# Block 2, MLA and sparse attention: values of two heads in turn, and ScalarE's order around the next head's exponentials

## The chip, the cores and the metric

The kernel runs on one NeuronCore of a Trainium2 chip. Its engines are TensorE (PE, matmuls; its weight loads stand apart as PEld), VectorE (DVE), ScalarE (ACT), GpSimd (POOL) and SyncE (SP), which issues DMAs. The engines run their own queues in order and wait for one another by semaphores. The metric is the time of one execution on the device in microseconds (us). Three runs of the kernel before took 2497.37, 2497.81 and 2498.92, median 2497.81.

## What is computed

Two transformer-like blocks of two layers each on 256 tokens of width 1024, all in fp32. Block 2 is the one that the change touches. In each of its layers four branches (MLA, a short convolution, sparse attention or DSA, gated linear attention or GLA) read the normed input; their outputs are merged with gates:

```python
merged = gates[:, :, 0, :] * (branches[0] @ w_branch[l, 0])
for n in range(1, N_BRANCH_2):
    merged = merged + gates[:, :, n, :] * (branches[n] @ w_branch[l, n])
```

MLA and DSA are attentions of four heads with values of width 64. For each head:

```python
s = jnp.einsum('bqhd,bkhd->bhqk', qb, k).astype(jnp.float32) * scale
s = jnp.where(key_pos[None, :] <= qpos[:, None], s, NEG)
p = jax.nn.softmax(s, axis=-1).astype(v.dtype)
return jnp.einsum('bhqk,bkhd->bqhd', p, v)
```

DSA does the same over 64 keys chosen by an index score, here as a mask over all keys; its values are shared by the heads.

## The kernel before

**Weights.** All weight matrices come through a ring of six slabs of eight 128x128 blocks. SyncE loads a slab when TensorE has released the one six places before; ScalarE copies it rounded to fp32r (`feed_slab`, line 879: "hi"), VectorE subtracts to get the rest ("lo", `low_slab`, line 1318; called lowering below), and TensorE multiplies hi by hi, hi by lo and lo by hi (line 456). ScalarE's `feed` stands behind an evacuation and copies up to four slabs ahead of it; VectorE's `low(..., 2)` goes two slabs ahead of the product it is about to read.

**Gate and branch products.** A merge step `merge2(n, j)` is a gate product "mA" (8 blocks, 24 matmuls of 256 columns) and a branch product "mB" (2 blocks, 6 matmuls). ScalarE takes the tanh of mA (`merge_sigmoid2`), then feeds a slab; VectorE multiplies (`merge_two`, lines 1776 and 1779). These products fill TensorE while attention goes through the other engines. In MLA's stage they are those of the convolution branch (n=1), in DSA's those of GLA (n=3), in GLA's those of MLA (n=0). Below, product k stands for the stage's `merge2(n, k)`.

**Attention of a head.** In block 2's MLA stage (and likewise DSA's) four engines share the work of head h:
- TensorE: scores of head h+1 (`attention_scores`), product 2h, transposes of head h's weights (`attention_turn`, waits for VectorE's "w"), product 2h+1, a wait for "tr" (the turned copy), and `values2`: two fp32 matmuls, which the trace shows as four, of 128 input rows and 64 output columns, writing partitions 0-63 (even head) or 64-127 (odd head) of one bank.
- VectorE: `attention_masked(h+1)` (lines 1746 to 1755, or 1750 in DSA), merge 2h, `attention_combined(h+1)` (reciprocal and weights, lines 1761 and 1766; waits for the exponentials and signals "w"), merge 2h+1, and behind an odd head `attention_output` (the split at lines 1304 and 1306). In MLA the GLA decays (lines 1928 to 1939, 1352) stand behind head 0 and their factors (line 1360) behind head 2; no slab is lowered in them.
- ScalarE: `attention_exp(h+1)` (waits for VectorE's "sc"), tanh of product 2h and a feed, `attention_turned(h)` (copy of the transposes to SBUF, whose drain at line 1166 signals "tr"), tanh of product 2h+1 and a feed.

The order is written out by hand in the loops over heads. PSUM has eight banks, and `b2.take` hands them out in turn: a tile gets the bank that was taken eight takes earlier, once its reader has freed it. GLA's values go through `values2` too, one head at a time. SS and SC2 hold two heads, at h % 2.

Of the kernel before, what the change touches and what calls it, by code (L numbers as in the profile page):

```python
# [34 lines left out]
P = 128  # L35
# [6 lines left out]
T2 = SEQ  # L42
# [175 lines left out]
def program(nc, x_meta, w, par1, lb, lam, final1, par2, positions, final2, consts, out, known):  # L218


    with ExitStack() as ctx:
# [139 lines left out]
        VM, a = view(a, 2, MLA_HEADS * 64)  # L361
# [8 lines left out]
        VS, a = view(a, 2, 64)  # L370
# [14 lines left out]
        GV, a = view(a, 2, GLA_HEADS * 64)  # L385
# [64 lines left out]
        def _(pe):  # L450
# [299 lines left out]
                transposes(b2, (kind, "t", h), [(slice(0, P), slice(i * P, (i + 1) * P), w[:, i * P:(i + 1) * P])  # L750
                                                for i in range(3)])

            def values2(kind, h, V):

                key = (kind, "o", h if kind == "g" else h // 2)
                ps = b2.take(pe, key) if h % 2 == 0 or kind == "g" else b2.of(key)
                r = slice(64 * (h % 2), 64 * (h % 2) + 64)
                mm(ps[r, 0:T2], V[:, 0, h * 64:h * 64 + 64] if V is not VS else V[:, 0, :], SS[:, h % 2, 0:T2], True, False)
                mm(ps[r, P:T2], V[:, 1, h * 64:h * 64 + 64] if V is not VS else V[:, 1, :], SS[:, h % 2, T2:3 * P], False, True,
                   b2.filled(key) if h % 2 or kind == "g" else None)  # L760

            def index_scores(i):

# [8 lines left out]
            for layer in range(DEPTH):  # L772
                enter("two", layer)
                products_behind_norm(b2, ("cq0", "cq1", "ckv"), hn2, T2, [s2["hn"].upto(("att", k)) for k in range(KT)],
                                     [s2["hnlo"].upto(("att", k)) for k in range(KT)])
                for key in ("iq0", "iq1", "ik"):
                    product(b2, key, hn2, T2)
                sum_squares(b2, "ss_q", [SQ2[:, i, :] for i in range(2)], T2, [s2["evac"].upto(k) for k in ("cq0", "cq1")])
                sum_squares(b2, "ss_kv", [SQ2[:, 2, :]], T2, [s2["evac"].upto("ckv")])
                for key in ("vsw", "kr"):  # L780
                    product(b2, key, hn2, T2)
                pe.wait_ge(*s2["evac"].upto("vsw"))
                transposes(b2, "vsw_turned", [(slice(0, P), slice(t * P, t * P + 64 + IDX_HEADS), VW[0:64 + IDX_HEADS, t * P:(t + 1) * P])
                                              for t in range(2)])
                index_scores(0)
                for key in ("cb0", "cc0"):
                    product(b2, key, hn2, T2)
                index_scores(1)
                for key in ("cb1", "cc1", "cx0", "cx1", "qs0", "qs1"):
                    product(b2, key, hn2, T2)  # L790
                pe.wait_ge(*s2["cqn"].upto())
                for h in range(MLA_HEADS):
                    product(b2, ("qu", h), [(CQS[0][:, k, :], CQS[1][:, k, :]) for k in range(2)], T2)
                pe.wait_ge(*s2["ckn"].upto())
                for h in range(MLA_HEADS):
                    product(b2, ("ku", h), [CKS], T2)
                token_major([("vu", 0), ("vu", 1)], [CKS])
                product(b2, "ks", hn2, T2)
                pe.wait_ge(*s2["evac"].upto("kr"))
                scores(b2, "kturn", [(slice(0, MLA_QK), slice(0, T2), rotM[0:MLA_QK, 0:MLA_QK], KR[0:MLA_QK, :])])  # L800
                for p in range(2):
                    pe.wait_ge(*s2["evac"].upto(("qu", 2 * p + 1)))
                    scores(b2, ("qturn", p), [(slice(0, MLA_QK), slice(i * T2, (i + 1) * T2), rotM[0:MLA_QK, 0:MLA_QK],
                                               QM[0:MLA_QK, 2 * p + i, :]) for i in range(2)])
                for key in ("glr", "gq", "gk", "gr0"):
                    product(b2, key, hn2, T2)
                pe.wait_ge(*s2["km"].upto())
                attention_scores("m", 0)
                token_major([("gv", 0), ("gv", 1)], hn2)
                pe.wait_ge(*s2["gls"].upto())  # L810
                product(b2, "gl", [GLS], T2)
                product(b2, "gr1", hn2, T2)
                for h in range(MLA_HEADS):
                    if h + 1 < MLA_HEADS:
                        attention_scores("m", h + 1)
                    merge2(1, 2 * h)
                    attention_turn("m", h)
                    merge2(1, 2 * h + 1)
                    pe.wait_ge(*s2["tr"].upto(("m", h)))
                    values2("m", h, VM)  # L820
                pe.wait_ge(*s2["z"].upto())
                for p in range(GLA_HEADS // 2):
                    pair = [(g, slice(32 * g, 32 * g + 32)) for g in (2 * p, 2 * p + 1)]
                    for t in range(2):
                        side_by_side(b2, [(("lv", g, t), level_parts(g, Z2[r, :, :], t, GQ[r, :], GK[r, :])) for g, r in pair])
                        if t == 1:
                            side_by_side(b2, [(("cross", g), [(slice(0, P), slice(0, P), Z2[r, 3, 0:P], Z2[r, 3, P:T2])]) for g, r in pair])
                        merge2(0, 4 * p + t)
                    if p == 1:
                        attention_scores("s", 0)  # L830
                    for g, r in pair:
                        merge2(0, 4 * p + 2 + g % 2)
                        pe.wait_ge(*s2["att"].upto(g))
                        values2("g", g, GV)
                    sum_squares(b2, ("ssg", p), [SQ2[:, p, :]], T2, [s2["sqo"].upto(p)], ones64)
                for h in range(DSA_HEADS):
                    if h + 1 < DSA_HEADS:
                        attention_scores("s", h + 1)
                    merge2(3, 2 * h)
                    attention_turn("s", h)  # L840
                    merge2(3, 2 * h + 1)
                    pe.wait_ge(*s2["tr"].upto(("s", h)))
                    values2("s", h, VS)
                for j in range(KT):
                    merge2(2, j)
                for j in range(KT):
                    product(b2, ("wo", j), [(Y2S[0][:, k, :], Y2S[1][:, k, :]) for k in range(KT)], T2,
                            ready=[s2["yb"].upto(k) for k in range(KT)] if j == 0 else None)
                sum_squares(b2, "ss_ffn", [Q2[:, 0, :], Q2[:, KT - 1, :]], T2,
                            [s2["total"].upto("ffn"), s2["sq"].upto(("ffn", KT - 1))])  # L850
                up = [("ff", j, half) for j in range(FT) for half in range(2)]
                products_behind_norm(b2, up[:3], hn2, T2, [s2["hn"].upto(("ffn", k)) for k in range(KT)],
                                     [s2["hnlo"].upto(("ffn", k)) for k in range(KT)])
                for key in up[3:]:
                    product(b2, key, hn2, T2)
                for j in range(KT):
                    product(b2, ("down", j), [(FF2[0][:, k, :], FF2[1][:, k, :]) for k in range(FT)], T2,
                            ready=[s2["ff"].upto(k) for k in range(FT)] if j == 0 else None)
                sum_squares(b2, "ss_next", [Q2[:, 0, :], Q2[:, KT - 1, :]], T2,
                            [s2["total"].upto("next"), s2["sq"].upto(("next", KT - 1))])  # L860
                stream["n"] += 1

        @block.scalar
        def _(act):
# [321 lines left out]
            for layer in range(DEPTH):  # L1186
# [57 lines left out]
                op(GE[:, :], GE[:, :], ACT.Ln, bias=one)  # L1244
                nc.scalar.drain().then_inc(*s2["gez"].done())
                for h in range(MLA_HEADS):
                    if h + 1 < MLA_HEADS:
                        attention_exp("m", h + 1)
                    merge_sigmoid2(1, 2 * h)
                    attention_turned("m", h)  # L1250
                    merge_sigmoid2(1, 2 * h + 1)
                    if h == 1:
                        act.wait_ge(*s2["zdiff"].upto())
                        op(Z2[:, :, :], Z2[:, :, :], ACT.Exp)
                        nc.scalar.drain().then_inc(*s2["zexp"].done())
# [13 lines left out]
                                     s2["ckn"].upto() if g == 1 else s2["normed"].upto(0))  # L1269
                attention_exp("s", 0)  # L1270
                for h in range(DSA_HEADS):
                    if h + 1 < DSA_HEADS:
                        attention_exp("s", h + 1)
                    merge_sigmoid2(3, 2 * h)
                    attention_turned("s", h)
                    merge_sigmoid2(3, 2 * h + 1)
                for j in range(KT):
                    merge_sigmoid2(2, j)
# [894 lines left out]
```

## Time and profile before

| | us |
|---|---|
| median of three runs | 2497.81 |
| the profiled execution | 2496.82 |
| its span, first to last instruction | 2495.0 |
| TensorE busy (matmuls) | 2354.8 |
| VectorE busy | 1807.5 |
| ScalarE busy | 1308.6 |

The profiled execution's own time is 1.8 above its span. A busy engine is one that executes; waiting instructions aren't busy. TensorE's matmuls overlap one another at their ends, so their busy time isn't a measure of full rate. The granted clock is 1.00 at 2.4 GHz and 0.50 at 1.2 GHz; its mean over the span was 0.982.

### The profile page before, as it was taken

Reading aid. Unit: us, or ns where it says so; the run is one execution under the profiler, and the core shown is the slowest. Engines: PE = TensorE matmul, PEld = TensorE weight load, DVE = VectorE, ACT = ScalarE, POOL = GpSimd, SP = SyncE. Lnnn points to the kernel's source line nnn. Section 1 sums busy time; section 2 is a strip of 40 time slices with the busy share of each in tenths; the row PEclk is TensorE's granted clock in tenths of the full one; section 3 lists DMA queues with packets and bytes.
Section 4 is the critical chain, followed back from the end, with each engine's and each line's share of the span. In section 5 each row is a group of like instructions: output and inputs, shape, how many; then the busy total and the mean of one; then the engine's idle time right before and its main releaser. Section 6 shows DMA issues by size and latency. Waiting matters only on the chain.

```text
span 2495.0 us, 51424 instructions
## 1 busy us (share of the span) xinstructions
PE 2354.8 (94%) x19438; PEld 2260.7 (91%) x19438; DVE 1807.5 (72%) x3521; ACT 1308.6 (52%) x2192; POOL 387.1 (16%) x492
## 2 busy tenths in 40 slices
PE   7999999998999999999998997989999988998998
PEld 6998898898999998899898997978999988888998
DVE  6689857777875689867777875887766558776764
ACT  5655456755544645556755545545443455455443
POOL 0000003626920000002727910000000000000000
PEclk9999999999999999999999998999999999999999
DMA  6433343344554433343344553433545544344553
GB/s 213 161 112 110 111 144 119 119 161 142 173 177 156 166 119 111 105 157 121 118 164 150 181 183 127 148 123 119 169 163 184 186 139 136 124 136 159 179 181 132
DMA packets 100436, 366.67 MB, mean 147 GB/s; under 512 B 11632, under 2 KB 12144, under 8 KB 99824
## 3 DMA queue, kind: packets, MB, share of 16 engines
q1 hardware_dynamic: 100208, 363.53, 43.5%
q8 instruction: 155, 2.54, 0.4%
q14 instruction: 73, 0.60, 0.1%
HBM read 362.44 MB, written 1.05 MB: 146 GB/s over the span
## 4 chain that ended last, share of the span: by engine, by line
PE 61%; DVE 22%; DVEq 5%; ACT 4%; issue 4%; ACTq 1%; DMA 1%; SPq 0%
PE psum L456 61%; DVE ring_lo L1318 5%; ACT arena L866 2%; DVE arena L1360 1%; DVE arena L1352 1%; DVE arena_r L1306 1%; DMA ring<-w 1%; ACT ring_hi L879 1%; DVE arena_r L1304 1%; DVE arena L1540 1%; PE psum L533 1%; DVEq L1804 1%; DVEq L1298 1%; DVE arena L1537 1%; DVE arena L1368 1%
## 5 line engine op out<-in xcount | busy, mean ns | idle before, releaser
L456 PE MATMUL psum<-hn_hi,ring_hi 128*128 128x272 f32 (+2 forms) x3936 | 1161.2, 296 | 47.5 <-ACT hn_hi L866 20.5
L456 PE MATMUL psum<-hn_hi,ring_lo 128*128 128x272 f32 (+2 forms) x3936 | 1132.5, 289 | 0.0
L456 PE MATMUL psum<-hn_lo,ring_hi 128*128 128x272 f32 (+2 forms) x3936 | 1096.2, 286 | 0.0
L1318 DVE TENSOR_TENSOR ring_lo<-ring,ring_hi 128x1024 fp32r<-128x1024 f32 x562 | 688.8, 1234 | 232.9 <-ACT ring_hi L879 191.0
L456 PEld LDWEIGHTS psum<-hn_hi,ring_hi 128*128 128x128 f32 x3936 | 760.1, 193 | 75.1 <-issue 50.3
L879 ACT ACTIVATE ring_hi<-ring 128x1024 fp32r<-128x1024 f32 x684 | 713.7, 1055 | 215.2 <-DMA ring<-w 185.0
L456 PEld LDWEIGHTS psum<-hn_hi,ring_lo 128*128 128x128 f32 x3936 | 760.8, 193 | 0.0
L456 PEld LDWEIGHTS psum<-hn_lo,ring_hi 128*128 128x128 f32 x3936 | 738.7, 191 | 1.6
L866 ACT ACTIVATE arena<-psum 128x272 f32<-128x272 f32 (+8 forms) x736 | 257.3, 367 | 652.0 <-PE psum L456 533.3
L456 PE MATMUL psum<-arena_r,ring_hi 128*128 128x256 f32 (+2 forms) x2996 | 552.6, 285 | 11.3 <-DVE arena L1854 6.4
L2017 POOL TENSOR_TENSOR ring_lo<-ring,ring_hi 128x256 fp32r<-128x256 f32 x488 | 386.9, 829 | 1060.3 <-ACT ring_hi L879 1060.2
L456 PEld LDWEIGHTS psum<-arena_r,ring_hi 128*128 128x128 f32 x2996 | 464.0, 189 | 15.0 <-DVE arena L1854 6.8
L456 PE MATMUL psum<-arena_r,ring_lo 128*128 128x256 f32 (+2 forms) x1498 | 424.1, 283 | 0.0
L456 PEld LDWEIGHTS psum<-arena_r,ring_lo 128*128 128x128 f32 x1498 | 282.6, 189 | 0.0
L456 PE MATMUL psum<-arena 128*64 128x64 f32 (+12 forms) x2464 | 195.3, 265 | 12.8 <-ACTq L1166 11.6
L456 PEld LDWEIGHTS psum<-arena 128*64 128x64 f32 (+6 forms) x2464 | 149.6, 153 | 58.0 <-issue 19.3
L866 ACT ACTIVATE arena<-arena 128x272 f32<-128x272 f32 (+9 forms) x151 | 87.7, 602 | 96.2 <-DVEq L1298 91.3
L1306 DVE TENSOR_TENSOR arena_r<-arena,arena_r 128x256 fp32r<-128x256 f32 (+2 forms) x150 | 81.4, 543 | 12.6 <-issue 1.7
L866 ACT ACTIVATE arena<-arena,small 128x128 f32<-128x128 f32 (+1 forms) x128 | 59.3, 464 | 55.4 <-DVEq L1298 53.2
L866 ACT ACTIVATE arena<-psum,par_sb 128x272 f32<-128x272 f32 (+1 forms) x88 | 49.6, 566 | 55.9 <-PE psum L456 55.7
L533 PE MATMUL psum<-cst,arena 128*128 128x128 f32 (+4 forms) x292 | 50.1, 273 | 27.6 <-ACTq L941 21.0
L456 PE MATMUL psum<-arena,cst 128*128 128x272 f32 (+2 forms) x232 | 71.1, 403 | 4.4 <-ACTq L1266 3.8
(159 smaller groups left out, 1433.0 us busy)
## 6 DMA issues: line engine op xcount, KB each, us to landing
ring<-w SPq DMA_DIRECT2D x684, 512.0 KB, 3.3
cst<-consts SPq DMA_DIRECT2D x1, 1960.0 KB, 14.0
x_sb<-x_meta SPq DMA_DIRECT2D x1, 1088.0 KB, 4.9
out<-x_sb SPq DMA_DIRECT2D x1, 1024.0 KB, 3.9
arena<-lam SPq DMA_DIRECT2D x1, 256.0 KB, 4.2
par_sb<-par SPq DMA_DIRECT2D x1, 193.0 KB, 4.8
pos_sb<-positions SPq DMA_DIRECT2D x1, 128.0 KB, 6.3
cst<-consts SPq DMA_DIRECT2D x1, 65.5 KB, 4.7
```

Of the source, the lines that this page charges most:

```text
L456: i = nc.tensor.matmul(out_, lhsT=lhsT, rhs=rhs, start=first, stop=last)
L533: t = nc.tensor.transpose(ps[rows, cols], src, ident[0:src.shape[0], 0:src.shape[0]])
L866: i = nc.scalar.activation(out_, in_, func, **kw)
L879: nc.scalar.activation(ring_hi[:, slot], ring[:, slot], ACT.Copy).then_inc(slab_hi[k % RING], 1)
L1298: i = V.drain()
L1304: V.tensor_copy(hi, src)
L1306: return V.tensor_tensor(lo, src, hi.bitcast(F32), ALU.subtract)
L1318: V.tensor_tensor(ring_lo[:, slot], ring[:, slot], ring_hi[:, slot].bitcast(F32), ALU.subtract)\
L1352: V.tensor_tensor(zq[:, z, 0:n].rearrange("p (b t s) -> p b t s", t=2, s=s), paired(C, s, n // (2 * s), step + s), paired(C, s, n // (2 * ...
L1360: V.tensor_tensor(d, d, paired(k, s, n // (2 * s), step + s), ALU.mult)
L1368: V.tensor_tensor(Lt[:, :, :], ps[:, 0:7 * HALF].rearrange("p (a b) -> p a b", b=HALF), lvl[:, :, :], ALU.mult)
L2017: i = nc.gpsimd.tensor_tensor(ring_lo[:, part], ring[:, part], ring_hi[:, part].bitcast(F32), ALU.subtract)
```

## The change

`values2` is replaced by two functions. `gla_values(g)` issues for GLA what was issued before. `pair_values(kind, p, V)` takes the bank of a pair and issues the four matmuls of both heads alternately: first half of keys for the even head, for the odd head, second half for the even head, for the odd head; the last one signals. It is called behind every odd head, when the turned copies of both are waited for, and nothing of the values stands behind an even head. On ScalarE the tanh of product 2h with its feed and the turned copy of head h go ahead of the exponentials of head h+1, in MLA and in DSA. VectorE's, GpSimd's and SyncE's orders are the same.

```diff
@@ -750,14 +750,21 @@
                 transposes(b2, (kind, "t", h), [(slice(0, P), slice(i * P, (i + 1) * P), w[:, i * P:(i + 1) * P])
                                                 for i in range(3)])
 
-            def values2(kind, h, V):
-
-                key = (kind, "o", h if kind == "g" else h // 2)
-                ps = b2.take(pe, key) if h % 2 == 0 or kind == "g" else b2.of(key)
-                r = slice(64 * (h % 2), 64 * (h % 2) + 64)
-                mm(ps[r, 0:T2], V[:, 0, h * 64:h * 64 + 64] if V is not VS else V[:, 0, :], SS[:, h % 2, 0:T2], True, False)
-                mm(ps[r, P:T2], V[:, 1, h * 64:h * 64 + 64] if V is not VS else V[:, 1, :], SS[:, h % 2, T2:3 * P], False, True,
-                   b2.filled(key) if h % 2 or kind == "g" else None)
+            def gla_values(g):
+
+                r = slice(64 * (g % 2), 64 * (g % 2) + 64)
+                ps = b2.take(pe, ("g", "o", g))
+                mm(ps[r, 0:T2], GV[:, 0, g * 64:g * 64 + 64], SS[:, g % 2, 0:T2], True, False)
+                mm(ps[r, P:T2], GV[:, 1, g * 64:g * 64 + 64], SS[:, g % 2, T2:3 * P], False, True, b2.filled(("g", "o", g)))
+
+            def pair_values(kind, p, V):
+
+                ps = b2.take(pe, (kind, "o", p))
+                for i, cols, src in ((0, slice(0, T2), slice(0, T2)), (1, slice(P, T2), slice(T2, 3 * P))):
+                    for e in range(2):
+                        h = 2 * p + e
+                        mm(ps[64 * e:64 * e + 64, cols], V[:, i, h * 64:h * 64 + 64] if V is not VS else V[:, i, :], SS[:, e, src],
+                           i == 0, i == 1, b2.filled((kind, "o", p)) if i and e else None)
 
             def index_scores(i):
 
@@ -816,8 +823,10 @@
                     merge2(1, 2 * h)
                     attention_turn("m", h)
                     merge2(1, 2 * h + 1)
-                    pe.wait_ge(*s2["tr"].upto(("m", h)))
-                    values2("m", h, VM)
+                    if h % 2:
+                        for g in (h - 1, h):
+                            pe.wait_ge(*s2["tr"].upto(("m", g)))
+                        pair_values("m", h // 2, VM)
                 pe.wait_ge(*s2["z"].upto())
                 for p in range(GLA_HEADS // 2):
                     pair = [(g, slice(32 * g, 32 * g + 32)) for g in (2 * p, 2 * p + 1)]
@@ -831,7 +840,7 @@
                     for g, r in pair:
                         merge2(0, 4 * p + 2 + g % 2)
                         pe.wait_ge(*s2["att"].upto(g))
-                        values2("g", g, GV)
+                        gla_values(g)
                     sum_squares(b2, ("ssg", p), [SQ2[:, p, :]], T2, [s2["sqo"].upto(p)], ones64)
                 for h in range(DSA_HEADS):
                     if h + 1 < DSA_HEADS:
@@ -839,8 +848,10 @@
                     merge2(3, 2 * h)
                     attention_turn("s", h)
                     merge2(3, 2 * h + 1)
-                    pe.wait_ge(*s2["tr"].upto(("s", h)))
-                    values2("s", h, VS)
+                    if h % 2:
+                        for g in (h - 1, h):
+                            pe.wait_ge(*s2["tr"].upto(("s", g)))
+                        pair_values("s", h // 2, VS)
                 for j in range(KT):
                     merge2(2, j)
                 for j in range(KT):
@@ -1244,10 +1255,10 @@
                 op(GE[:, :], GE[:, :], ACT.Ln, bias=one)
                 nc.scalar.drain().then_inc(*s2["gez"].done())
                 for h in range(MLA_HEADS):
+                    merge_sigmoid2(1, 2 * h)
+                    attention_turned("m", h)
                     if h + 1 < MLA_HEADS:
                         attention_exp("m", h + 1)
-                    merge_sigmoid2(1, 2 * h)
-                    attention_turned("m", h)
                     merge_sigmoid2(1, 2 * h + 1)
                     if h == 1:
                         act.wait_ge(*s2["zdiff"].upto())
@@ -1269,10 +1280,10 @@
                                      s2["ckn"].upto() if g == 1 else s2["normed"].upto(0))
                 attention_exp("s", 0)
                 for h in range(DSA_HEADS):
+                    merge_sigmoid2(3, 2 * h)
+                    attention_turned("s", h)
                     if h + 1 < DSA_HEADS:
                         attention_exp("s", h + 1)
-                    merge_sigmoid2(3, 2 * h)
-                    attention_turned("s", h)
                     merge_sigmoid2(3, 2 * h + 1)
                 for j in range(KT):
                     merge_sigmoid2(2, j)
```

## Rows read from the trace of the kernel before

**Rows 1.** The page: part 1, and the engines in the chain that ended last.
```profile
PE 2354.8 (94%) x19438; PEld 2260.7 (91%) x19438; DVE 1807.5 (72%) x3521; ACT 1308.6 (52%) x2192; POOL 387.1 (16%) x492
...
PE 61%; DVE 22%; DVEq 5%; ACT 4%; issue 4%; ACTq 1%; DMA 1%; SPq 0%
```

**Rows 2.** TensorE's waits: waiter, releaser: us in total, times, longest.
```profile
PE psum L456 <- ACTq L1166: 11.6, 6, 2.4
...
PE psum L456 <- DVE arena_r L1306: 3.6, 4, 1.3
```

**Rows 3.** MLA's stage, layer 0: window, us, busy by engine, clock, DMA.
```profile
1626.80:1669.00 42.20, 34.34 (x251) 31.49 (x251) 32.55 (x72) 21.78 (x38) 0.00 (x0) 0.96 0.34 113
```

**Rows 4.** TensorE's timeline in MLA's stage, layer 0: start, us, instruction [idle before].
```profile
1647.92 1.72 PE L456 MATMUL psum<-arena 128*64 128x256 f32 x8 [2.41 <-ACTq L1166]
...
1650.60 0.58 PE L456 MATMUL psum<-hn_hi,ring_hi 128*128 128x256 f32 x1 [0.96 <-DVE arena_r L1306]
...
1659.71 0.86 PE L456 MATMUL psum<-arena 128*64 128x256 f32 x4
1660.51 0.39 PE L456 MATMUL psum<-hn_hi,ring_hi 128*128 128x256 f32 x1
```

**Rows 5.** ScalarE's timeline, layer 0: MLA's stage, then DSA's.
```profile
1644.76 0.40 ACT L866 ACTIVATE arena<-arena,small 128x128 f32<-128x128 f32 x1 [5.93 <-DVEq L1298]
...
1647.36 0.47 ACT L866 ACTIVATE arena<-psum 128x384 f32<-128x384 f32 x1
...
1719.05 0.40 ACT L866 ACTIVATE arena<-arena,small 128x128 f32<-128x128 f32 x1 [3.36 <-DVEq L1298]
...
1720.18 1.28 ACT L866 ACT_TABLE_LOAD   x1
1721.47 0.38 ACT L866 ACTIVATE arena<-psum 128x256 f32<-128x256 f32 x1
1721.97 1.06 ACT L879 ACTIVATE ring_hi<-ring 128x1024 fp32r<-128x1024 f32 x1
1722.93 0.47 ACT L866 ACTIVATE arena<-psum 128x384 f32<-128x384 f32 x1
```

**Rows 6.** TensorE's timeline, block 1: level products of one tile.
```profile
123.64 1.14 PE L456 MATMUL psum<-arena 128*64 128x64 f32 x30
```

**Rows 7.** TensorE's timeline in DSA's stage: layer 0 twice, layer 1.
```profile
1723.49 1.71 PE L456 MATMUL psum<-arena 128*64 128x256 f32 x8 [1.67 <-ACTq L1166]
...
1736.89 0.39 PE L456 MATMUL psum<-hn_hi,ring_hi 128*128 128x256 f32 x1 [0.85 <-DVE arena_r L1306]
...
2215.04 0.39 PE L456 MATMUL psum<-hn_hi,ring_hi 128*128 128x256 f32 x1 [0.50 <-DVE arena_r L1306]
```

**Rows 8.** VectorE's timeline in MLA's stage: layer 0, the last row layer 1.
```profile
1635.35 0.17 DVE L1761 RECIPROCAL small<-small 128x2 f32<-128x2 f32 x1 [0.20 <-issue]
...
1644.81 1.23 DVE L1318 TENSOR_TENSOR ring_lo<-ring,ring_hi 128x1024 fp32r<-128x1024 f32 x1
...
1646.36 0.42 DVE L1776 SCALAR_TENSOR_TENSOR arena<-arena,psum 128x256 f32<-128x256 f32 x1 [0.32 <-ACTq L1174]
...
1655.97 0.42 DVE L1776 SCALAR_TENSOR_TENSOR arena<-arena,psum 128x256 f32<-128x256 f32 x1 [1.13 <-PE psum L456]
...
1659.89 0.42 DVE L1776 SCALAR_TENSOR_TENSOR arena<-arena,psum 128x256 f32<-128x256 f32 x1 [1.17 <-PE psum L456]
...
1668.38 0.42 DVE L1776 SCALAR_TENSOR_TENSOR arena<-arena,psum 128x256 f32<-128x256 f32 x1 [1.87 <-PE psum L456]
...
2135.97 0.42 DVE L1776 SCALAR_TENSOR_TENSOR arena<-arena,psum 128x256 f32<-128x256 f32 x1 [2.50 <-PE psum L456]
```

**Rows 9.** TensorE's weight loads in GLA's stage, layer 0.
```profile
1684.80 0.19 PEld L456 LDWEIGHTS psum<-hn_hi,ring_hi 128*128 128x128 f32 x1 [0.15 <-DVE ring_lo L1318]
```

**Rows 10.** Behind DSA's first values, layers 0 and 1: columns as rows 3.
```profile
1725.20:1728.60 3.40, 3.40 (x18) 3.40 (x18) 2.98 (x6) 1.86 (x5) 0.00 (x0) 0.54 0.02 5
...
2205.20:2208.20 3.00, 3.00 (x26) 3.00 (x26) 2.58 (x6) 1.67 (x4) 0.00 (x0) 1.00 0.00 0
```

## The prediction

> **What bounds the kernel now.** I read the page first: TensorE (PE) is busy in 94% of the span and most of the chain that ended last is its matmuls [rows 1], so a microsecond is gained only where TensorE stands still or where its own instructions go. The list of waits comes next: TensorE stood 11.6 us, six times, for line 1166, the drain behind ScalarE's copy of turned weights, and 3.6 us, four times, for VectorE's split at line 1306 [rows 2]. I then looked where these fall. All are in the MLA and sparse (DSA) stages of block 2, two layers each, so four stages. In the first, TensorE is busy in 34.34 of 42.20 us [rows 3]: 7.9 us idle. The timeline shows the pattern there: values of a head start after idle 2.41, the product behind them after 0.96 more [rows 4]. In each of the four stages the values of head 0 wait (1.66 to 1.72), and in both MLA stages those of head 1 as well (2.41, 2.42).
>
> ScalarE is why. Its queue has exp(h+1), tanh, a weight slab's copy, then the turned copy. In MLA exp(2) stood 5.93 us for VectorE (masking comes behind its long GLA block), with tanh and turned(1) queued behind it, and turned(1) ran only at 1647.36. In DSA exp(1) came after 3.36 of idling, then table load 1.28, tanh, slab copy, turned(0) at 1722.93 [rows 5].
>
> **The change, part by part.**
>
> *Values.* A head's values now take 0.80 from their first matmul to the next product's first (1659.71 to 1660.51) [rows 4]. Values of heads 0 and 2 leave their place: head 0's takes 0.80 with it (a switch to the score matmuls stays), head 2's 0.80 and the switch in front, 0.09 (start to start 0.21 where products have 0.12). That is 1.69 per stage. Against it a pair is longer than one head. It has 8 passes of 1536 columns. If halves of the array don't overlap: 0.80 is 768 columns plus a switch of 0.17, so 0.82 ns a column, and the pair is 1.26 + 0.17 = 1.43, +0.63. If they do: the level products write partitions 0-63 and 64-127 in turn with all 128 input rows, just as the pair will, and 30 passes of 64 columns took 1.14 with the last one's 0.22 of drain in it [rows 6], 0.031 a pass, 0.48 ns a column, where one behind the other they would be 0.053 and 1.6 in all. So weights of one half load while the other half streams, and the pair is 0.74 + 0.17 = 0.91, +0.11. I take 0.1: same tile shape, same alternation, only wider. Bounds per pair: 0 and +0.63; 8 pairs.
>
> The Trainium skill says otherwise (TensorE: Matmul & The Clock Gate, Part 3, "What overlaps and what doesn't"): weight loads overlap running matmuls only when the row group differs, and the two heads share all rows. By that rule the pair would be the serial one; it is the first rival.
>
> *Waits for turned copies, and the order on ScalarE.* tanh(2h) and turned(h) no longer sit behind exp(h+1). Even heads' waits go with their values. For h=1, tanh(2) can run as its gate product ends, turned(1) behind the transposes: about 1640.4 in layer 0's MLA, and TensorE comes to the pair at 1642.8. No wait; TensorE is first there. The split's waits (0.96, 1.31 [its pattern in layer 0: rows 4], 0.85, 0.50 [rows 7]) were for a PSUM bank: banks go round in eights and gate product 4 got that of pair 0's values. With the pair taken later, product 4 gets the bank of scores 2, freed by masking, and pair 0's bank comes due at product 6's second half. That wait goes as well.
>
> What is late next differs by stage.
>
> *MLA, both layers: VectorE.* It has the long GLA block and no slab is lowered in it; TensorE lives on two slabs of lead. Rolled forward in layer 0, with 2.9 for a gate product (24 matmuls at 0.12), 0.7 for its branch product, 0.25 for transposes, 0.8 for scores with their switch: TensorE leaves product 1 at 1634.5, does scores 2, product 2, turn 1 and product 3 by 1642.8, the pair by 1643.7, scores 3 by 1644.5, and after one block of product 4 stands at the next slab at 1645.0. VectorE lowered that slab from 1644.81 on [rows 8], now 0.6 later (below), so it ends near 1646.6; TensorE waits 1.6 there. From then VectorE is the chain and gains just its old idling: 0.32 + 1.13 + 1.17 + 1.87 [rows 8] + 0.30 at the last split = 4.8. The new order costs it one wait: combined(1) started at 1635.35 [rows 8]; now table load, tanh, slab copy, turned(0) and exp(1) run first (ScalarE is free at 1631.5; 1.28 + 0.4 + 1.1 + 0.5 + 1.1), to 1635.9: 0.6. Net 4.2. In layer 1 the same with 2.50 [rows 8] for 1.13: 5.6. TensorE itself would be 5.7 and 7.3 ahead at the stage's end, but GLA takes this back: in the old trace TensorE already stood 0.15 for a lowering there [rows 9], so that slab has no slack and the gain is VectorE's. The falls of the granted clock in these stages are thereby covered too and I count nothing for them.
>
> *DSA, both layers: TensorE.* Two heads cost it about 9 us, VectorE 7.5 to 8. Rolled forward in layer 0 by the same steps: TensorE leaves product 1 at 1721.7, has scores 2 by 1722.8, product 2 by 1726.5, turn 1 and product 3 by 1730.3. The pair needs turned(1): ScalarE has tanh 2 at 1725.9, a slab copy, and turned(1) by 1727.7, 2.6 early. Turns want w(1) at 1726.5 (VectorE has it at 1723.3) and w(3) at 1743.5 (1739.1). exp(h+1) now starts only after turned(h), 1.5 after the gate product; VectorE is late by more than that with its lowerings, so I find one wait of 0.25 on it, inside TensorE's lead. Layer 0: 1.67 + 0.85 [rows 7] + 1.69 - 0.2 = 4.0, and the clock: after the idling it fell to 1.2 GHz, mean 0.54 for 3.40 us in which 18 matmuls ran, where layer 1 at full clock (2.4 GHz) had 26 in 3.00 [rows 10]; 18 are 2.1, so 1.3 is lost. Without the idling I expect no fall: 5.3. Layer 1, without one: 1.66 + 0.50 + 1.69 - 0.2 = 3.65.
>
> No DMA, slab or table load is added or moved; slab copies stay behind the same tanh, up to a few us earlier, and the slab transfers follow TensorE's releases, earlier by what TensorE gains.
>
> **Sum.** 4.2 + 5.6 + 5.3 + 3.65 = 18.8. Span 2495.0 - 18.8 = 2476.2; the profiled execution took 1.8 more than its span, 2478.0, and the median of the runs shown is 1.0 above that execution: 2479.0.
>
> **Rivals.**
> 1. *The pair doesn't overlap* (it doesn't do what it says). In MLA +0.63 hides behind VectorE; in DSA 4 pairs cost 0.53 more than counted: 2481.1. The level products speak against it, unless long streams behave otherwise.
> The Trainium skill's rule on weight loads, named above, would give that time too.
> 2. *Idle moves and the clock falls elsewhere.* MLA has a new wait of 1.6 beside narrow matmuls, and TensorE meets VectorE anew in GLA. A fall costs 1.3 to 1.5 if nothing covers it. Two to four falls more, with VectorE's later waits not all absorbed (half of MLA's 9.8 lost): 2479 + 4.9 + 4 = 2488. For it: falls already sit behind such idling [rows 10]. Against: total idling shrinks.
> 3. *Slower: VectorE waits at every combined(h+1).* exp(h+1) now ends about 3.2 after the gate product, VectorE's merge at 1.8 if it is prompt; so it waits 1.4, lowers its next slab that much later, and if TensorE has no lead, stands for it. Three heads, four stages: 12 x 1.4 = 16.8 lost, with the gain consumed by the same chain: 2497.8 + 16.8 = 2514.6. It decides where VectorE comes to combined less than 1.4 behind the merge and TensorE's lead is under one slab. Rows 8 show VectorE idling before merges 4, 5 and 7, that is prompt, in the old order; but there its lead was two slabs, and once TensorE stops waiting VectorE isn't prompt.
> 4. *Unseen gain*: neither the 0.6 in MLA nor pair cost, and one clock fall elsewhere goes: 2476.
>
> **How the numbers follow.** Forecast with its neighbours (2475 to 2483): 0.58, within it; rival 1: 0.12; rival 2: 0.15; rival 4 or beyond (down to 2472): 0.08; rival 3 whole or in part: 0.07, of which 0.04 ends slower. About 0.2% (5.0 us) is what a measurement here can tell from no change. Faster than 2492.8 has the forecast, rivals 1, 2 and 4, less a hundredth of rival 2: 0.92; within it 0.04; slower 0.04. The range reaches to rival 2's end and a little under rival 4: 2473 to 2489.
>
> **What would show it.** Line 1166 gone from TensorE's list of waits, or near; values as eight matmuls with their starts in pairs a few ns apart, four times in each layer; line 1306 not releasing product 4; in MLA VectorE with next to no idling between the GLA block and pair 1, and TensorE's idling there named after ring_lo (line 1318); granted clock 1.00 at DSA's start in layer 0. Wrong if the starts of a pair's matmuls are 0.2 apart throughout, if VectorE shows waits for ScalarE line 1159 in all heads, or if TensorE idles as much as before under other names.

## The result, and the profile after

The changed kernel took 2478.64 us (median of four runs, 2478.29 to 2480.0) beside 2498.36 for the kernel before on the same chip: ratio 0.992, 95% interval 0.9903 to 0.9938, 0.8% or 19.7 us faster. The profiled execution's span is 2476.9 against 2495.0. Forecast were 2479.0 and 18.8 us. Lines behind the edit on TensorE's side stand 11 further down (L1166 is now L1177, L1306 is L1317, L1318 is L1329, L1159 is L1170).

The page of the changed kernel, part 1 and the engines of the chain, answers to [rows 1]:

```profile
PE 2345.0 (95%) x19438; PEld 2253.9 (91%) x19438; DVE 1806.4 (73%) x3521; ACT 1306.9 (53%) x2192; POOL 386.6 (16%) x492
...
PE 60%; DVE 23%; DVEq 6%; ACT 4%; issue 4%; DMA 1%; ACTq 1%; SPq 0%
```

In TensorE's list of waits both rows of [rows 2], the turned copy's and the split's, are gone. In their place the waits for a lowered slab have grown (before: 20.1 us, 19 times), and there is a small new one, for the masking:

```profile
PE psum L456 <- DVE ring_lo L1329: 26.9, 25, 3.3
...
PE psum L456 <- DVE arena L1758: 0.4, 2, 0.2
```

TensorE's timeline in MLA's stage, layer 0, answers to [rows 4]. All its idling from the transposes of head 0 to GLA stands in it: a slab (1.58, the same as before the change), the bank of scores 2 (0.21), product 4's second slab (1.43). The windows view behind it has the first pair alone (the ninth matmul of x9 is the end of the product before):

```profile
1634.24 0.39 PE L456 MATMUL psum<-hn_hi,ring_hi 128*128 128x256 f32 x1 [1.58 <-DVE ring_lo L1329]
...
1643.67 1.72 PE L456 MATMUL psum<-arena 128*64 128x256 f32 x12
...
1645.60 0.39 PE L456 MATMUL psum<-hn_hi,ring_hi 128*128 128x256 f32 x1 [0.21 <-DVE arena L1758]
...
1647.65 0.39 PE L456 MATMUL psum<-hn_hi,ring_hi 128*128 128x256 f32 x1 [1.43 <-DVE ring_lo L1329]
```

```profile
1643.66:1644.46 0.80, 0.80 (x9) 0.49 (x8) 0.80 (x4) 0.00 (x0) 0.00 (x0) 1.00 0.57 225
```

VectorE and ScalarE there, for [rows 8] and [rows 5]: one wait for exp(1), 1.27; behind the GLA block VectorE's merges have no idling in front (pair 1's starts at 1665.67), and turned(1) runs at 1640.82, ahead of the 5.02 that exp(2) stands for masking:

```profile
1636.92 0.17 DVE L1772 RECIPROCAL small<-small 128x2 f32<-128x2 f32 x1 [1.27 <-ACTq L1170]
...
1646.37 1.23 DVE L1329 TENSOR_TENSOR ring_lo<-ring,ring_hi 128x1024 fp32r<-128x1024 f32 x1
1647.51 0.41 DVE L1787 SCALAR_TENSOR_TENSOR arena<-arena,psum 128x256 f32<-128x256 f32 x1
...
1655.90 0.41 DVE L1787 SCALAR_TENSOR_TENSOR arena<-arena,psum 128x256 f32<-128x256 f32 x1
...
1663.32 0.41 DVE L1787 SCALAR_TENSOR_TENSOR arena<-arena,psum 128x256 f32<-128x256 f32 x1
```

```profile
1640.82 0.47 ACT L877 ACTIVATE arena<-psum 128x384 f32<-128x384 f32 x1
1646.31 0.40 ACT L877 ACTIVATE arena<-arena,small 128x128 f32<-128x128 f32 x1 [5.02 <-DVEq L1309]
```

GLA's slab, for [rows 9] (TensorE's weight loads; the matmul behind it shows 0.77), and DSA's start in layer 0 at full clock, for [rows 10]:

```profile
1681.38 0.19 PEld L456 LDWEIGHTS psum<-hn_hi,ring_hi 128*128 128x128 f32 x1 [0.97 <-DVE ring_lo L1329]
```

```profile
1718.36:1721.76 3.40, 3.40 (x26) 3.07 (x26) 2.91 (x8) 1.90 (x2) 0.00 (x0) 1.00 0.45 159
```

**By stages.** Both traces hold the same 16,410 product matmuls in the same order, so the start of one in a trace less its start before is how far that kernel is ahead there, and the change of this over a stage is what the stage gained. This is worked out from the starts, for the changed kernel and every experiment (us; negative is faster):

```
                      MLA 0  GLA 0  DSA 0  MLA 1  GLA 1  DSA 1    sum   time  before  ratio (95%)
changed               -5.20  +0.80  -5.91  -6.57  +0.79  -4.07 -20.16 2478.64 2498.36 0.9920 (0.9903-0.9938)
e9_changed_again      -5.21  +0.83  -5.89  -6.90  +1.12  -4.07 -20.12 2479.27 2499.44 0.9924 (0.9910-0.9938)
e1_pairs_only         -1.08  +0.01  -5.59  -3.43  -0.01  -3.75 -13.85 2488.53 2496.09 0.9968 (0.9956-0.9980)
e2_order_only         +0.22  -0.01  -2.77  -0.96  -0.02  -0.94  -4.48 2495.15 2496.09 0.9995 (0.9986-1.0004)
e3_head_by_head       -5.20  +0.77  -5.89  -6.60  +0.78  -4.05 -20.19 2479.18 2496.09 0.9927 (0.9913-0.9940)
e4_exp1_before_feed   -6.59  +1.11  -5.91  -7.98  +1.08  -4.07 -22.36 2482.18 2496.09 0.9940 (0.9925-0.9955)
e10_exp1_again        -6.59  +1.13  -5.91  -7.95  +1.13  -4.08 -22.27 2476.80 2499.44 0.9912 (0.9899-0.9926)
e5_mla_only           -5.20  +0.78  -1.48  -6.91  +1.11  -0.01 -11.71 2488.24 2498.48 0.9962 (0.9946-0.9977)
e6_dsa_only           +0.08  +0.01  -5.88  -0.93   0.00  -4.09 -10.81 2488.17 2498.48 0.9959 (0.9944-0.9974)
e7_even_twice         -5.50  +1.11  -4.51  -6.89  +1.12  -2.67 -17.34 2485.76 2498.48 0.9947 (0.9932-0.9962)
e8_gpsimd_lowers      -6.32  +1.11  -5.89  -7.59  +0.75  -4.07 -22.01 2479.87 2498.48 0.9929 (0.9915-0.9942)
```

Outside these stages the changed kernel's trace lost 1.0 early in block 1, 2.4 between the layers and gained 1.3 behind the last stage, where falls of the granted clock lie in one trace and not in the other: -20.2 + 1.0 + 2.4 - 1.3 = -18.1, the difference of the spans. Where TensorE is the chain and no fall lies in a stage, the stages repeat within 0.04 (DSA layer 1: -4.05 to -4.09 in the seven traces with pairs and order both changed there). MLA alone moves by up to 0.3 between traces of one kernel (layer 1: -6.57 and -6.90), and GLA behind it gives that back (together -5.78 both times). The times, with such falls in them, move by 3, so the experiments are read by stages first. One thing goes into every row of the table: all are compared with the same single trace of before, and falls in that trace count as a gain. Two of them are found below, 1.48 in DSA of layer 0 (e5) and 0.93 in MLA of layer 1 (e6), so of each sum about 2.4 (an estimate from these two entries) isn't shown to be the change's work. Of the 20.2, some 17.8 is left.

### The profile page after: what moved, and what is told of

It reads as the page before. It is cut to its first block, busy times and chain, and to the rows that moved or that the text cites. A ratio compares the mean times of both kernels' runs of the same rounds, so it can differ in the third digit from the quotient of the medians.

```text
span 2476.9 us, 51424 instructions
## 1 busy us (share of the span) xinstructions
PE 2345.0 (95%) x19438; PEld 2253.9 (91%) x19438; DVE 1806.4 (73%) x3521; ACT 1306.9 (53%) x2192; POOL 386.6 (16%) x492
## 4 chain that ended last, share of the span: by engine, by line
PE 60%; DVE 23%; DVEq 6%; ACT 4%; issue 4%; DMA 1%; ACTq 1%; SPq 0%
PE psum L456 59%; DVE ring_lo L1329 5%; ACT arena L877 2%; DVE arena L1371 2%; DVE arena L1363 1%; DMA ring<-w 1%; DVE arena_r L1317 1%; ACT ring_hi L890 1%; DVE arena_r L1315 1%; DVE arena L1551 1%; DVE arena L1379 1%; DVEq L1788 1%; PE psum L533 1%; DVEq L1815 1%; DVEq L1309 1%
## 5 line engine op out<-in xcount | busy, mean ns | idle before, releaser
L1329 DVE TENSOR_TENSOR ring_lo<-ring,ring_hi 128x1024 fp32r<-128x1024 f32 x562 | 688.6, 1233 | 237.7 <-ACT ring_hi L890 196.1
L456 PE MATMUL psum<-arena 128*64 128x64 f32 (+13 forms) x2464 | 188.7, 265 | 1.2 <-ACTq L1053 1.0
L456 PEld LDWEIGHTS psum<-arena 128*64 128x64 f32 (+7 forms) x2464 | 146.4, 154 | 43.1 <-issue 18.6
L1317 DVE TENSOR_TENSOR arena_r<-arena,arena_r 128x256 fp32r<-128x256 f32 (+2 forms) x150 | 81.2, 541 | 12.6 <-issue 1.7
```

The lines of the kernel that those rows point to most:

```text
L456: i = nc.tensor.matmul(out_, lhsT=lhsT, rhs=rhs, start=first, stop=last)
L1317: return V.tensor_tensor(lo, src, hi.bitcast(F32), ALU.subtract)
L1329: V.tensor_tensor(ring_lo[:, slot], ring[:, slot], ring_hi[:, slot].bitcast(F32), ALU.subtract)\
```

## The experiments

Four questions: which half of the change brings what, why a pair costs nothing, which engine sets MLA's end, and whether the clock's fall belonged to the idling.

### e1_pairs_only: TensorE's side alone

```diff
-                    merge_sigmoid2(1, 2 * h)
-                    attention_turned("m", h)
                     if h + 1 < MLA_HEADS:
                         attention_exp("m", h + 1)
+                    merge_sigmoid2(1, 2 * h)
+                    attention_turned("m", h)
```
(against the changed kernel, and the same in DSA)

> TensorE's side of the change alone: values of two heads in one pair behind every odd head, ScalarE's order as before (exponentials of the next head first). Theory (pairs are what helps in DSA, the order what helps in MLA): in DSA the pair needs only turned(1), which ScalarE has some 1.5 us before TensorE gets there even behind exp(2), so no wait for line 1170's copy there and DSA gains as in the whole change, 5.9 in layer 0 and 4.1 in layer 1. In MLA exp(2) stands for the masking behind VectorE's long GLA block with turned(1) behind it, so TensorE waits at pair 0 until about the same moment as before, 5 us or more in one piece; only the wait for the split and the values of head 2 are gained, about 2 per layer. Sum 14, time 2484.5. Rival (ScalarE's order is the main part in all stages): DSA keeps waits for turned copies at the pairs, gains under 2 per stage, time 2491 or more. Rival (the order adds nothing, pairs are all): 2479, as the whole change.

The sum was -13.9, 14 expected; the time was 2488.53, 4.0 above the expected 2484.5. In DSA TensorE waits 0.26 and 0.25 for a turned copy, so the order of ScalarE is worth 0.3 a stage there. In MLA it stands 5.19 in one piece behind product 3, as foreseen. TensorE's timeline of this kernel, layer 0's MLA and DSA:

```profile
1645.60 3.13 PE L456 MATMUL psum<-arena 128*64 128x256 f32 x12 [5.19 <-ACTq L1177]
...
1727.21 1.72 PE L456 MATMUL psum<-arena 128*64 128x256 f32 x12 [0.26 <-ACTq L1177]
```

Per stage I was off in MLA: 1.1 gained in layer 0 where 2 were expected, 3.4 in layer 1. In layer 0 more of the stage ran at 1.2 GHz, mean granted clock 0.87 (0.96 before, [rows 3]); windows view of that stage:

```profile
1624.50:1662.70 38.20, 31.77 (x225) 30.24 (x226) 30.86 (x70) 20.49 (x36) 0.00 (x0) 0.87 0.33 111
```

The time, 7.6 less than before, fell short of the stages' sum: the trace lost 4.7 between the layers, and gained 2.3 ahead of the first MLA stage.

### e2_order_only: ScalarE's side alone

```diff
-                    if h + 1 < MLA_HEADS:
-                        attention_exp("m", h + 1)
                     merge_sigmoid2(1, 2 * h)
                     attention_turned("m", h)
+                    if h + 1 < MLA_HEADS:
+                        attention_exp("m", h + 1)
```
(against the kernel before, and the same in DSA)

> ScalarE's side alone: tanh, feed and turned(h) ahead of exp(h+1), TensorE's values head by head in their old places. Theory: the six waits for turned copies go, but in both layers' MLA product 4 still takes the bank of pair 0's values and waits for VectorE's split, which comes no earlier (VectorE has no idling up to there), so MLA gains nothing or loses 0.5 a layer; DSA layer 0 gains its 1.7 wait and the clock fall behind it, 1.9, DSA layer 1 its 1.7; the 0.9 and 0.5 for the split and all values stay. Sum 4 to 5.3, time 2493 to 2494.5. Rival (the waits for turned copies are the loss, whatever the values do): all 11.6 us of them plus the clock, 2485.

The sum came out as expected, -4.5, but 2.4 of it is the falls in the trace of before that every row shares, which leaves about 2.1. The time says the same: 2495.15 where 2493 to 2494.5 was expected, 0.9 less than before, and the interval of the ratio holds 1. So ScalarE's order alone isn't a gain clear of noise. What holds of the theory is the wait that comes next. The waits for turned copies shrink from 11.6 to 0.6, and the one for the split takes their place, from 3.6 to 13.0. TensorE's list of waits, then its timeline in layer 0's MLA and DSA:

```profile
PE psum L456 <- DVE arena_r L1306: 13.0, 4, 5.4
...
PE psum L456 <- ACTq L1166: 0.6, 2, 0.3
```

```profile
1651.61 0.58 PE L456 MATMUL psum<-hn_hi,ring_hi 128*128 128x256 f32 x1 [5.03 <-DVE arena_r L1306]
...
1735.17 0.39 PE L456 MATMUL psum<-hn_hi,ring_hi 128*128 128x256 f32 x1 [1.28 <-DVE arena_r L1306]
```

So neither half does it alone. The raw sums, 13.9 and 4.5, make 18.3, 1.8 less than the whole, but they hold the 2.4 of before's trace twice. Without it the halves are about 11.4 and 2.1, together 13.5 of 17.8: some 4.2 comes only when both are there. The times on this chip agree in direction (7.6 and 0.9 for the halves, 16.9 for e3, which has both). Taking the pair late is what frees product 4 of the split's bank.

### e3_head_by_head: the order inside a pair

```diff
-                for i, cols, src in (...):
-                    for e in range(2):
-                        h = 2 * p + e
+                for e in range(2):
+                    h = 2 * p + e
+                    for i, cols, src in (...):
```

> The changed kernel, but inside a pair all four passes of the even head come before the four of the odd head. Theory (it is the alternation between partitions 0-63 and 64-127 that makes a pair as short as one head, 0.80): head by head a pair takes about 1.4, +0.6; in MLA that lies inside TensorE's waits for lowered slabs (1.4 behind pair 0, 0.8 in GLA), in DSA it is lost in full, four pairs x 0.6 = 2.4; time 2481. If TensorE were the chain in MLA as well it would be 8 x 0.6 = 4.8: 2483.4. Rival (the order inside a pair doesn't matter, the array takes both halves at once in any order): 0.80 a pair, 2478.6.

My theory fell: all stages are as in the changed kernel. By shapes, the passes that start in the pair's first 0.47 us (1643.63 to 1644.10) and in the rest of it (the line with ring_lo is the end of the product before); columns as in the costliest groups of the page:

```profile
L456 PE MATMUL psum<-arena 128*64 128x256 f32 x4 | 0.7, 405 | 0.0
L456 PE MATMUL psum<-arena_r,ring_lo 128*128 128x256 f32 x1 | 0.3, 279 | 0.0
...
L456 PE MATMUL psum<-arena 128*64 128x128 f32 x4 | 0.4, 273 | 0.0
```

Issued were two passes of 256 columns and two of 128 for the even head, then as many for the odd. Four of 256 start first: the odd head's ran ahead of the even head's 128-wide ones, and its first started 14 ns behind the even head's first. Halves run beside one another whatever the order of issue.

### e7_even_twice: the same half twice

```diff
-                for i, cols, src in (...):
-                    for e in range(2):
+                for e in (0, 0, 1):
+                    for i, cols, src in (...):
```

> The changed kernel, but in every pair the even head's two matmuls are issued twice before the odd head's, the second time over the first. Theory (halves of the array's columns run beside one another in whatever order they are issued, the same half one behind the other): the repeat needs the same half, 768 columns more, so a pair takes 0.80 + 0.6 = 1.4; in MLA the waits for lowered slabs behind the pairs (1.4 and 0.8) hide it, in DSA it is lost: 4 x 0.6 = 2.4, time 2481. Rival (matmuls of 64 output columns overlap whatever half they write): 0.8 a pair, no loss. Rival (TensorE is the chain in MLA as well): 8 x 0.6 = 4.8.

The pair now spans 1.50 (1644.62 to 1646.12), 0.70 more: the same half does queue. Passes that start in the first 0.63 us, the even head's alone:

```profile
L456 PE MATMUL psum<-arena 128*64 128x256 f32 x2 | 0.6, 405 | 0.0
L456 PE MATMUL psum<-arena 128*64 128x128 f32 x2 | 0.4, 272 | 0.0
```

The odd head's first starts only with the even head's fifth (1645.33 and 1645.32), so the overtaking reaches over three waiting passes, here as in e3. Over four it didn't: when the even head's fourth started (1645.21), four of its passes still waited, and the odd head's first with them. DSA lost 1.40 in each layer, 0.70 a pair (expected 0.6). MLA with GLA lost nothing: -4.39 and -5.77 beside -4.40 and -5.78. That settles that TensorE isn't the chain in MLA. The time, 2485.76, is 4.8 above the expected 2481: outside the stages this trace lost 6.1, the changed kernel's 2.1.

### e4_exp1_before_feed, e10_exp1_again and e9_changed_again: VectorE's wait for exp(1)

```diff
-                    merge_sigmoid2(1, 2 * h)
+                    merge_sigmoid2(1, 2 * h, feeds=h > 0)
+                    if h == 0:
+                        attention_exp("m", 1)
+                        feed(b2, ("mA", 1, 0))
                     attention_turned("m", h)
-                    if h + 1 < MLA_HEADS:
+                    if 0 < h < MLA_HEADS - 1:
                         attention_exp("m", h + 1)
```

> The changed kernel, but behind head 0 of MLA ScalarE does tanh, exp(1), slab copy, turned(0) in place of tanh, slab copy, turned(0), exp(1). Theory (VectorE is the chain in MLA, and its 1.27 us wait for exp(1) at combined(1) is on it): exp(1) ends 1.5 earlier, combined(1) starts about 1.1 earlier in each layer, product 4's wait for its slab shrinks by as much, and both layers' MLA and GLA together gain 1.1: 2476.4 by the times, 2.2 less than the changed kernel. Rival (that wait is hidden, TensorE is the chain): no difference from the changed kernel, 2478.6. Rival (the slab copy, now 1.1 later, is what VectorE waits for next): under 0.3 gained.

VectorE's timeline of this kernel has nothing left of the 1.27 but the 0.20 of issue:

```profile
1634.72 0.17 DVE L1776 RECIPROCAL small<-small 128x2 f32<-128x2 f32 x1 [0.20 <-issue]
```

MLA with GLA gained 5.48 and 6.90, 1.1 more in each layer, as the theory says. The time didn't show it (2482.18), so both were run once more beside one another:

> The changed kernel once more, beside the version with exp(1) ahead of the slab copy, on the same chip. Every account: its stages against the kernel before as in its first profile (MLA with GLA -4.4 and -5.8, DSA -5.9 and -4.1, each within 0.1 where no fall of the granted clock lies in only one of the two), the time within 3 us of 2478.6, since falls elsewhere of 1.3 to 1.5 each come and go.

> The same kernel as the run with exp(1) ahead of the slab copy. Theory (VectorE's wait for exp(1) is on the chain in MLA): MLA with GLA -5.5 and -6.9 again, 2.2 less in all than the changed kernel beside it, in the time as in the trace if falls of the clock elsewhere don't cover it. Rival (the first profile's 1.1 a layer was chance): the stages as in the changed kernel.

The stages repeated, and the times were 2476.80 and 2479.27, 2.5 apart. The intervals of the two ratios overlap; what carries it is the stages' 2.2, twice. By the stages it is the fastest version found; by the times it was so on one chip and 3.0 slower than e3, whose stages are the changed kernel's, on the other.

A rival has to be met here. The changed kernel has a stretch at 1.2 GHz in layer 0's MLA (mean granted clock 0.96 from 1626.80 to 1664.80), and e4 and e10 have none there (1.00), so the 1.1 might be the clock's. It isn't: e7 has none there either (1.00 from 1628.00 to 1665.00), and its MLA with GLA gained 4.39, the changed kernel's 4.40.

### e5_mla_only and e6_dsa_only: one stage at a time

The diffs are the change's own hunks for "m" or for "s", the other stage left with `values2` and the old order.

> The whole change in the MLA stages alone (pairs and ScalarE's order); DSA as before. Theory (the stages don't lean on one another): MLA with the GLA stage behind it gains 4.4 in layer 0 and 5.8 in layer 1, as in the changed kernel, DSA nothing; the old wait of 1.67 and the fall of the granted clock behind DSA's first values are back in layer 0. Sum 10.2, time some 2488. Rival (part of DSA's gain came from MLA, as TensorE arrives earlier there): DSA moves by more than 0.3.

> The whole change in the DSA stages alone; MLA as before. Theory: 5.9 in layer 0, 4.1 in layer 1, MLA nothing: sum 10.0, time some 2488. In layer 0 the clock fall behind the first values is gone. Rival (the fall goes because of what happens earlier, in MLA): it stays, and layer 0 gains 1.9 less, 4.0.

Both times came as expected. The stages don't lean on one another, but two entries that should be nothing aren't. In e5 DSA of layer 0, unchanged, gained 1.48: its wait was there and no fall of the clock behind it (TensorE's timeline, then the window from that start, at 2.4 GHz throughout):

```profile
1718.83 1.71 PE L456 MATMUL psum<-arena 128*64 128x256 f32 x8 [1.66 <-ACTq L1183]
```

```profile
1718.80:1722.20 3.40, 3.37 (x22) 2.71 (x23) 2.98 (x7) 2.39 (x3) 0.00 (x0) 1.00 0.10 35
```

In e6 MLA of layer 1, unchanged, gained 0.93, and in e2, with its new order, 0.96: the execution of before had more time at 1.2 GHz there. Windows view of that stage, before and in e6; e2 has 0.92 as well:

```profile
2105.40:2149.00 43.60, 36.85 (x253) 34.00 (x253) 32.55 (x72) 21.79 (x38) 0.00 (x0) 0.88 0.33 110
...
2101.80:2144.50 42.70, 35.58 (x247) 32.82 (x248) 32.80 (x73) 21.40 (x38) 0.00 (x0) 0.92 0.32 111
```

Without these two the halves make 10.2 and 9.9, together 20.1, the whole's 20.2.

### e8_gpsimd_lowers: two of MLA's slabs to GpSimd

```diff
-              if a == 96 or k % 6 != 3}
+              if a == 96 or k % 6 != 3} | {432, 435, 572, 575}
```
(on top of e4)

> The kernel with exp(1) ahead of the slab copy, and in each layer's MLA stage two of the slabs for which TensorE waits (the one of 1.6 us behind head 0, and product 4's) are lowered by GpSimd in place of VectorE. Theory (VectorE is the chain in MLA and its own load is what is left): VectorE loses two slabs of 1.23; GpSimd, which takes 3.1 a slab, starts on them 7 and 5 us before they are due. A lowering on VectorE beside a GpSimd one takes 1.56 in place of 1.23 in block 1, so up to 0.8 a slab is given back: net 0.8 to 2.1 a layer, I take 1.5. MLA and GLA together gain 7.0 in layer 0 and 8.4 in layer 1 against the kernel before; time 2473.5. Rival (with both waits gone TensorE is the chain and its own matmuls bound the stage): the gain ends at the 1.1 of GLA's wait. Rival (contention takes all): as without GpSimd's slabs, 2476.4.

The rival that contention takes all holds: MLA with GLA -5.21 and -6.84 beside e4's -5.48 and -6.90, and the time was 2479.87 where 2473.5 was expected. GpSimd took the slabs in time, but VectorE's GLA decays beside it took up to 2.3 times as long (in e4 0.43, 0.29, 0.69 and 0.29 for the four rows), 1.6 in all. GpSimd's timeline, then VectorE's:

```profile
1639.57 3.46 POOL L2032 TENSOR_TENSOR ring_lo<-ring,ring_hi 128x256 fp32r<-128x256 f32 x4 [13.19 <-ACT ring_hi L890]
```

```profile
1639.61 0.98 DVE L1946 TENSOR_TENSOR arena<-arena 128x256 f32<-128x256 f32 x1
1640.68 0.66 DVE L1948 TENSOR_SCALAR arena<-arena 128x256 f32<-128x256 f32 x1
1641.41 1.08 DVE L1950 TENSOR_TENSOR_SCAN arena<-cst,arena 128x256 f32<-128x256 f32 x1
1642.57 0.61 DVE L1952 TENSOR_SCALAR arena<-arena 128x256 f32<-128x256 f32 x1
...
1648.64 0.17 DVE L1776 RECIPROCAL small<-small 128x2 f32<-128x2 f32 x1 [0.50 <-ACTq L1170]
```

VectorE's waits for ScalarE, which it now reached too early, took another 1.0 (0.67, 0.34 and 0.50 where e4 has 0.20, 0.12 and 0.18). Together that is a little more than the two slabs of 1.23. Ahead of the stage, beside GpSimd's first slab (1622.57 to 1626.38), VectorE's lowering took 1.62 in place of 1.22, and TensorE lost 0.41 before the stage's first product, which the table doesn't count in layer 0. VectorE's MAX8 and MATCH_REPLACE8 beside that slab took 0.43 and 0.41, as in e4. The Trainium skill (SBUF — State Buffer, Who interferes with whom) has it that VectorE and GpSimd share a pair of ports, held for a whole instruction, and names `tensor_scalar` among the operations that can contend in a two-port mode. The rows agree in that the operations with two inputs and the `tensor_scalar` ones both slow down; how long a port is held they leave open.

## Why the prediction was right

Per stage, forecast and measured: MLA with GLA layer 0 4.2 and 4.40, layer 1 5.6 and 5.78; DSA layer 0 5.3 and 5.91, layer 1 3.65 and 4.07. Sum 18.8 and 20.2; 2.1 was then lost outside the stages, so part of the closeness of 2479.0 to 2478.64 is luck. Another part is that forecast and stages were both reckoned from the same single trace of before: its two falls are some 2.4 of the 20.2 and, as 1.3 for DSA and a part of layer 1's 5.6, in the forecast too. The mechanism doesn't rest on them: the waits that were to go went, and the ones that were to come came.

- *Values.* The pair was to cost 0.1 more than a head. It costs nothing: 0.80 [rows 4], eight passes for four. Eight pairs, of which DSA's four count: 0.4 of the excess. The reason given, that alternation lets one half load while the other streams, was half right: the halves overlap, alternation isn't needed (e3).
- *Rest of DSA's excess,* 0.61 in layer 0 and 0.42 in layer 1. A wait costs slightly more than its idle: in e5 the values start 1.94 behind the last product pass where 0.21 is usual, 1.73 lost for an idle of 1.66. Two such waits a stage are 0.14. With the 0.2 a stage for the pairs, and in layer 0 the 0.2 by which the clock's term was short (below), that leaves under 0.1 a stage, whose cause stays open.
- *MLA's schedule* came out within 0.1 of the roll-forward up to the slab, with this trace's offset of 1.0 at the stage's start taken off: pair at 1642.7 (1642.8), the slab until 1646.7 (1646.6), combined(1) 0.58 later (0.6). TensorE's lead was less exact: 5.20 at MLA's end and 4.40 behind GLA (5.7 and 4.2), in layer 1 6.57 and 5.78 (7.3 and 5.6). Not foreseen: 0.21 for the bank of scores 2, ahead of a longer wait and so free.
- *VectorE is the chain in MLA*: shown from both sides. 0.70 a pair more on TensorE cost nothing (e7), 1.1 less on VectorE gave 1.1 (e4, e10).
- *DSA is TensorE's*: turned(1) was done at 1724.31, 2.6 ahead of the pair at 1726.88, as computed; adding to TensorE cost in full (e7).
- *The clock's* term had a reason that isn't shown. 1.3 was counted for the fall in DSA's layer 0, "without the idling I expect no fall". The fall is gone and is worth 1.5, but the change isn't shown to be the reason: e5 kept the idling and had no fall either. Of the twelve traces only the one of before has a fall there, and it is the only trace of that kernel. Much of layer 1's higher MLA term (VectorE's 2.50 of [rows 8] in place of 1.13) was likewise where falls happened to lie in the one execution that I read, 0.9 by e6.
- *Rivals.* 1, the serial pair, is refuted: 0.80 a pair, and the odd head's first weights begin to load at 1643.68, 5 ns into the even head's first pass. With it falls the rule of the Trainium skill that the prediction set against its own working (TensorE: Matmul & The Clock Gate, Part 3, "What overlaps and what doesn't"), that weight loads overlap only across row groups: both heads share all rows here. Another page of the Trainium skill (TensorEngine Tiling (Array Packing), Key Properties) lets tiles load and multiply independently, and that is what the rows show. 3: VectorE waited for an exponential in one head per MLA stage, not in all. 2: the falls of the clock moved, and their net outside the stages was 2.1 lost, less than its price; half of MLA's gain wasn't lost (4.40 and 5.78).

## What to carry to other kernels

Two 64-column matmul groups that write different halves of the partitions cost the time of one if they are issued close together, in either order: gather them, and let the wait they need stand late, where the bank they take also comes due later. Moving a producer ahead in a second engine's queue pays little (here about 2.1 by the stages, 0.9 in the time) while the consumer then meets the next releaser; ask what frees the bank. Where falls of the clock come and go in single executions, compare the start of the same instruction in two traces, stage by stage: that repeated to 0.04 us here in stages without a fall, where times of 2480 moved by 3. A single trace to compare with brings its own falls into every result, here some 2.4 of 20.2. An experiment that leaves a stage as it was shows them, so take a second trace of the kernel before, or keep such a stage as a control.

## What the runs showed of the hardware

- Passes of a half overtook three waiting passes of the other half, 14 ns behind its first (e3), but not four (e7). The Trainium skill (TensorE: Matmul & The Clock Gate, Part 3, "What overlaps and what doesn't") calls matmul starts strictly first in, first out; the four 256-wide starts of e3 ahead of any 128-wide one differ from that.
- The same half twice cost 0.70 for 768 columns more at 2.4 GHz, 0.91 ns a column.
- VectorE's fp32 operations on 256 columns took 0.61 to 1.08 beside a GpSimd subtraction, 0.29 to 0.69 alone (e8, e4), but MAX8 and MATCH_REPLACE8 were as fast as alone (0.43 and 0.41).
- A stretch at 1.2 GHz cost 1.5 where TensorE was the chain (DSA, e5 against before) and nothing where VectorE was (MLA with GLA, the changed kernel with one against e7 without: 4.40 and 4.39). Two executions of the changed kernel differ in where they have one: from 2064.80 to 2068.00 the granted clock was 0.50 in the first and 1.00 in e9.
